# Two attention mixers: rope rows swapped by SBUF to SBUF copies, and the latent up projection packed by parts

## The chip, the core and the metric

The kernel runs on one core of one Trainium2 chip. The time is that of the device, in microseconds, for one launch, as the median of repeated runs. It is lower for a better kernel. The input is one sequence of 512 tokens with 1024 features, in fp32.

## What the kernel computes

One layer with a gated delta rule and windowed attention comes first (not touched here), and then two identical layers, each made of a feed-forward block, a mixer, a second feed-forward block and a gated embedding block. The mixer is what changes. Cut to what matters, with x normalised, it is:

```
p = x @ w_in_2[l]                       # 1024 -> 384 latents, 32 shared rope key, 1024 dilated q and k, 512 dilated v
q_lat, kv_lat = norm(p[:, 0:256]), norm(p[:, 256:384])
q  = (q_lat @ w_q_up).reshape(512, 8, 96)       # per head 64 plain features and 32 that are rotated
kv = (kv_lat @ w_kv_up).reshape(512, 8, 128)    # per head 64 key features and 64 value features
key of head h   = [kv[:, h, 0:64], rope(p[:, 384:416])]      # 96 features; the rope part is shared by the heads
query of head h = [q[:, h, 0:64],  rope(q[:, h, 64:96])]
latent heads : softmax(causal(query . key / sqrt(96))) @ value, 8 heads
dilated heads: 8 heads of 64 features, 4 tiles of queries and 4 of keys (two heads to a tile), all rotated
rope(a) = a * cos + swapped(a) * signed sin     # swapped: rows i and i ^ 16 (latent) or i ^ 32 (dilated) change places
```

Features lie on the 128 partitions and tokens along the free axis, so a rotation has to exchange rows between partitions.

## The kernel before

All projections run as sums of three products (`matmul3`, lines 227 to 229): weights and activations are split into a high part (`w_hi`, made by ScalarE at line 181) and a rest (`w_lo`, made by VectorE at line 189). Weights come in granules of 128 by 1024 numbers (512 KB), fetched by SyncE at line 171 into one of four raw slots. Four split granules are kept. `w_split`, `w_used` and similar semaphores count granules, and every engine walks its own written order; there is no scheduler. In the last section of the program (`chain`) each engine simply runs the mixer's method of its name (`sp`, `pool`, `pe`, `act`, `dve`).

The mixer has three parts on TensorE:

- **Twelve input tiles** t, 24 products each. From t = 6 each is preceded by one rope swap. VectorE drains a tile by multiplying it with the reciprocal root (line 2655).
- **Twenty up tiles** j: 8 query tiles (one head each, 96 of 128 rows used, 6 products), 8 key tiles (64 of 128 rows used, 3 products), 4 value tiles (3 products). The first eleven are preceded by one swap each. ScalarE drains each tile (lines 2526, 2528 and 2530) into `qh`, `kh` and `vm`.
- **64 attention items** (`score`, `turn`, `weigh`), with 32 pieces of the dilated value product (`values`) between the first 32 of them.

A rotation ("rope") r goes as follows. TensorE multiplies the raw tile by a permutation matrix (`swap`, line 2330) into PSUM, GpSimd multiplies the raw tile by the cosines into `by_cos` (line 2310), VectorE multiplies the swapped tile by the signed sines into `by_sin` (line 2612) and adds the two (line 2617). There are 17 of them in each mixer: r = 0 the shared key, 1 to 4 dilated queries, 5 to 8 dilated keys, 9 to 16 the eight latent query heads. `by_cos` and `by_sin` have two slots each. GpSimd starts `by_cos` of r when the sum of r - 2 is done.

The first score waits for all up tiles to be drained. Here are its waits and those of `turn`, which end with the last rope:

```
if i < 16:
    pe.wait_ge(*self.rope_added(10 + head))
if i == 0:
    pe.wait_ge(*self.up_drained(self.UPS))
    pe.wait_ge(*self.key_copied(1))
```

Of the kernel before, what the change touches and what calls it, by code (L numbers as in the profile page):

```python
# [22 lines left out]
ALU = mybir.AluOpType  # L23
# [39 lines left out]
def _small(*fields):  # L63
# [17 lines left out]
    ("ffn0", 44 + 24), ("mix_in", 12), ("up", 4), ("mix_v", 4), ("mix_out", 8), ("ffn1", 44 + 24), ("ple", 3), ("ple_gate", 8))  # L81
# [2130 lines left out]
class Mixer:  # L2212
# [13 lines left out]
    def __init__(self, kit, layer, delta_gain, leave, b):  # L2226
        self.kit, self.layer, self.b, self.made, self.leave = kit, layer, b, leave.makes, leave
        self.g0, self.u0, self.v0, self.o0 = kit.take(self.TILES), kit.take(4), kit.take(4), kit.take(KD)
# [36 lines left out]
    def up_ready(self, j):  # L2265

        last_of = {3: 1, 7: 2, 15: 3, 19: 4}
        if j in last_of:
            return self.kit.w_used, self.u0 + last_of[j]
        return self.up_done(j + 1 - sum(e < j for e in last_of))  # L2270

    def rope_job(self, r):

        b = self.b
        if r == 0:
            return b["k_rope"][:, :], [(slice(0, P), b["k_rope"][:, :])], "swap_16", 0, self.drained(4)
        if r < 5:
            raw = self.kit.delta[:, 2 * (r - 1)]
            return raw, [(slice(0, HD), raw[0:HD]), (slice(HD, P), self.kit.delta[HD:P, 2 * (r - 1) + 1])], "swap_32", 1, self.drained(r + 4)
        if r < 9:  # L2280
            return b["kd"][:, r - 5], [(slice(0, P), b["kd"][:, r - 5])], "swap_32", 1, self.drained(r + 4)
        return b["qh"][:, r - 9], [(slice(0, P), b["qh"][:, r - 9])], "swap_16", 0, self.up_drained(r - 8)
# [8 lines left out]
    def sp(self, sp):  # L2291
# [5 lines left out]
        fetch_ahead(kit, sp, self.g0, self.TILES + 8 + KD)  # L2297

    def pool(self, pool):
# [5 lines left out]
        for r in range(self.ROPES):  # L2305
# [14 lines left out]
    def pe(self, pe):  # L2320
# [3 lines left out]

        def swap(r):
            src, _, name, _, ready = self.rope_job(r)
            pe.wait_ge(*ready)
            if r >= 2:
                pe.wait_ge(*self.sin_done(r - 1))
            pe.matmul(kit.banks[4 + r % 2][:, :], kit.square(name), src, start=True, stop=True).then_inc(self.swapped.sem, 1)  # L2330

        self.entry.pe(pe)
        for t in range(2, self.TILES):
# [19 lines left out]
            if t >= 6:  # L2353
                swap(t - 6)
# [6 lines left out]
        for j in range(self.UPS):  # L2361
            if j + 6 < self.ROPES:
                swap(j + 6)
            pe.wait_ge(*(self.drained(7 + j) if j < 4 else self.up_drained(j - 3)))
            if j in (0, 8):
                pe.wait_ge(*self.lat_rested(2 if j == 0 else 3))
            if j in (0, 4, 8, 16):
                pe.wait_ge(kit.w_split, u0 + (0, 4, 8, 16).index(j) + 1)
            out = self.up_bank(j)[:, :]
            if j < 8:  # L2370
                for k in range(2):
                    last = matmul3(pe, out, kit.w_tile(u0 + j // 4, j % 4 * 2 + k), [x[:, k] for x in lat], k == 0, k == 1)
            elif j < 16:
                last = matmul3(pe, out, kit.w_tile(u0 + 2, j - 8), [x[:, 2] for x in lat], True, True)
            else:
                tok = slice((j - 16) * P, (j - 15) * P)
                last = matmul3(pe, out, [x[:, 2, tok] for x in lat], kit.w_wide(u0 + 3, 0), True, True)
            last.then_inc(kit.w_used if j in (3, 7, 15, 19) else self.up_done.sem, 1)

        def score(i):  # L2380
# [40 lines left out]
        def turn(i):  # L2421
# [3 lines left out]
            else:  # L2425
                pe.wait_ge(*self.rope_added(self.ROPES))
# [64 lines left out]
    def act(self, act):  # L2491
# [26 lines left out]
        for j in range(self.UPS):  # L2518
            if j in (0, 4, 8, 16):
                kit.w_make_hi(act, self.u0 + 3 + (0, 4, 8, 16).index(j))  # L2520
            act.wait_ge(*self.up_ready(j))
            bank = self.up_bank(j)
            if j == 4:
                act.wait_ge(*self.lat_rested(3))
            if j < 8:
                last = act.activation(b["qh"][:, j], bank[:, :], ACT.Copy)
            elif j < 16:
                last = act.activation(b["kh"][0:HD, j - 8], bank[0:HD, :], ACT.Copy)
            else:
                last = act.activation(b["vm"][:, j - 16, :, 0:HD], bank[:, :].rearrange("p (h n) -> p h n", h=8), ACT.Copy)  # L2530
# [68 lines left out]
    def dve(self, dve):  # L2599
# [4 lines left out]
        def rope(r):  # L2604
            _, parts, _, table, _ = self.rope_job(r)
            dve.wait_ge(*self.swapped(r + 1))
# [5 lines left out]
            dve.tensor_tensor(by_sin, kit.banks[4 + r % 2][:, :], b["cos_sin"][:, 2 + table], ALU.mult).then_inc(  # L2612
# [341 lines left out]
def layer_buffers(kit):  # L2954
# [24 lines left out]
    place(EXIT_UNIT, ("probs_t", [P, 2, 512]))  # L2979
# [40 lines left out]
def pack_weights(x):  # L3020
# [34 lines left out]
    for l in range(LAYERS):  # L3055
# [11 lines left out]
        q_up = np.zeros((256, 8, P), w.dtype)  # L3067
        q_up[:, :, 0:96] = x["w_q_up_2"][l].reshape(256, 8, 96)
# [111 lines left out]
```

## Time and profile before

| | value |
|---|---|
| median of 3 runs | 3229.46 us (3228.98 to 3229.71) |
| the profiled execution, its own time | 3230.68 us |
| its span, first to last instruction | 3228.8 us |
| TensorE busy | 2996.9 us, 93% |
| VectorE, ScalarE, GpSimd busy | 49%, 36%, 10% |
| mean granted TensorE clock | 0.962 |
| SyncE's queue | 433 weight fetches of 512 KB |

The profiled execution took 1.2 us more than the median of the runs, and 1.9 us of its time lie outside the span. Busy time is what an engine spent in instructions. In the chain of work that ended last each moment is given to one engine, the one that everything behind it waited for. A matmul's record overlaps the next one's, so the chain's pieces, and not the records, tell what a product costs. "Idle before" a row tells how long that engine had nothing to do before it and what released it.

### The profile page before, as it was taken

Reading aid. Unit: us, or ns where it says so; the run is one execution under the profiler, and the core shown is the slowest. Engines: PE = TensorE matmul, PEld = TensorE weight load, DVE = VectorE, ACT = ScalarE, POOL = GpSimd, SP = SyncE. Lnnn points to the kernel's source line nnn. Section 1 sums busy time; section 2 is a strip of 40 time slices with the busy share of each in tenths; the row PEclk is TensorE's granted clock in tenths of the full one; section 3 lists DMA queues with packets and bytes.
Section 4 is the critical chain, followed back from the end, with each engine's and each line's share of the span. In section 5 each row is a group of like instructions: output and inputs, shape, how many; then the busy total and the mean of one; then the engine's idle time right before and its main releaser. Section 6 shows DMA issues by size and latency. Waiting matters only on the chain.

```text
span 3228.8 us, 39471 instructions
## 1 busy us (share of the span) xinstructions
PE 2996.9 (93%) x15600; PEld 2504.5 (78%) x15600; DVE 1580.6 (49%) x2589; ACT 1177.5 (36%) x1885; POOL 311.5 (10%) x293
## 2 busy tenths in 40 slices
PE   5988799889799999998999999899999989999997
PEld 2877689867678888766788888788888667888886
DVE  5725465442544443754464434654436645544336
ACT  4324544233232332434443323533324345423224
POOL 0001077600000000120100000000000200000000
PEclk8999899999899999998999999999999999999998
DMA  5220100012223232310123232133332201232331
GB/s 214 71 73 1 64 1 1 1 53 78 72 87 102 93 103 92 103 48 27 40 81 98 95 105 92 54 110 98 98 105 98 65 14 40 72 98 94 102 97 54
DMA packets 66854, 241.90 MB, mean 75 GB/s; under 512 B 7408, under 2 KB 9584, under 8 KB 66032
## 3 DMA queue, kind: packets, MB, share of 16 engines
q1 hardware_dynamic: 66672, 239.38, 22.8%
q8 instruction: 125, 2.05, 0.3%
q14 instruction: 57, 0.47, 0.0%
HBM read 236.21 MB, written 3.15 MB: 74 GB/s over the span
## 4 chain that ended last, share of the span: by engine, by line
PE 64%; DVE 4%; ACT 2%; issue 1%; DVEq 0%; ACTq 0%
PE pair L227 19%; PE pair L229 18%; PE pair L228 18%; PE pair L2417 2%; PE pair L2392 2%; PE pair L376 1%; PE pair L2429 1%; PE pair L2330 1%; ACT w_hi_at L181 1%; DVE rstd_at L500 1%; DVE work_at L331 1%; DVE w_lo_at L189 0%; ACT probs_t_at L2547 0%; DVE h_lo_at L340 0%; PE pair L518 0%
## 5 line engine op out<-in xcount | busy, mean ns | idle before, releaser
L227 PE MATMUL pair<-h_hi_at,w_hi_at 128*128 128x512 f32 (+1 forms) x2048 | 790.1, 386 | 35.2 <-DVE h_lo_at L340 30.8
L228 PE MATMUL pair<-h_lo_at,w_hi_at 128*128 128x512 f32 (+1 forms) x2048 | 761.7, 372 | 0.0
L229 PE MATMUL pair<-h_hi_at,w_lo_at 128*128 128x512 f32 (+1 forms) x2048 | 761.5, 372 | 0.0
L189 DVE TENSOR_TENSOR w_lo_at<-w_raw,w_hi_at 128x1024 fp32r<-128x1024 f32 x350 | 440.7, 1259 | 465.3 <-ACT w_hi_at L181 465.2
L181 ACT ACTIVATE w_hi_at<-w_raw 128x1024 fp32r<-128x1024 f32 x350 | 367.3, 1054 | 549.7 <-PE pair L229 538.4
L227 PEld LDWEIGHTS pair<-h_hi_at,w_hi_at 128*128 128x128 f32 x2048 | 391.0, 191 | 113.7 <-DVE h_lo_at L340 36.3
L228 PEld LDWEIGHTS pair<-h_lo_at,w_hi_at 128*128 128x128 f32 x2048 | 391.5, 191 | 70.5 <-issue 3.4
L229 PEld LDWEIGHTS pair<-h_hi_at,w_lo_at 128*128 128x128 f32 x2048 | 391.2, 191 | 65.3
L2181 DVE TENSOR_TENSOR work_at<-pair,rstd_at 128x512 f32<-128x512 f32 (+1 forms) x184 | 122.1, 667 | 362.9 <-PE pair L229 362.8
L227 PE MATMUL pair<-a_hi_at,w_hi_at 128*128 128x512 f32 (+1 forms) x792 | 290.1, 366 | 0.0
L228 PE MATMUL pair<-a_lo_at,w_hi_at 128*128 128x512 f32 (+1 forms) x792 | 289.4, 365 | 0.0
L229 PE MATMUL pair<-a_hi_at,w_lo_at 128*128 128x512 f32 (+1 forms) x792 | 289.4, 365 | 0.0
L508 POOL TENSOR_TENSOR exit_work_at<-exit_work_at 128x512 f32<-128x512 f32 x44 | 63.1, 1435 | 2222.2 <-ACT exit_work_at L470 2222.0
L227 PE MATMUL pair<-h_hi,w_hi 128*128 128x512 f32 (+1 forms) x432 | 166.3, 385 | 29.2 <-DVE h_lo L264 21.5
L2157 ACT ACTIVATE work_at<-work_at 128x512 f32<-128x512 f32 x88 | 55.7, 633 | 334.6 <-DVE work_at L2181 334.6
L227 PEld LDWEIGHTS pair<-a_hi_at,w_hi_at 128*128 128x128 f32 x792 | 149.4, 189 | 24.3
L228 PEld LDWEIGHTS pair<-a_lo_at,w_hi_at 128*128 128x128 f32 x792 | 149.3, 189 | 24.3
L229 PEld LDWEIGHTS pair<-a_hi_at,w_lo_at 128*128 128x128 f32 x792 | 149.3, 189 | 24.0
L228 PE MATMUL pair<-h_lo,w_hi 128*128 128x512 f32 (+1 forms) x432 | 163.6, 379 | 0.0
L229 PE MATMUL pair<-h_hi,w_lo 128*128 128x512 f32 (+1 forms) x432 | 163.1, 378 | 0.0
L189 DVE TENSOR_TENSOR w_lo<-w_raw,w_hi 128x1024 fp32r<-128x1024 f32 x59 | 71.9, 1225 | 185.0 <-ACT w_hi L181 184.9
L181 ACT ACTIVATE w_hi<-w_raw 128x1024 fp32r<-128x1024 f32 x59 | 62.1, 1060 | 216.5 <-PE pair L229 195.7
(394 smaller groups left out, 4371.0 us busy)
## 6 DMA issues: line engine op xcount, KB each, us to landing
w_raw<-in_weights SPq DMA_DIRECT2D x433, 512.0 KB, 3.5
residual<-in_x SPq DMA_DIRECT2D x1, 2048.0 KB, 11.7
cos_sin_at<-rope_table SPq DMA_DIRECT2D x2, 1024.0 KB, 5.3
out<-residual SPq DMA_DIRECT2D x16, 128.0 KB, 1.7
ctx_in<-in_ctx SPq DMA_DIRECT2D x1, 1024.0 KB, 12.9
rope_table<-zb SPq DMA_DIRECT2D x1, 1024.0 KB, 4.9
mask_at<-in_layer_masks SPq DMA_DIRECT2D x2, 512.0 KB, 6.4
levels<-in_levels SPq DMA_DIRECT2D x1, 896.0 KB, 7.3
```

What stands on the lines that cost most here:

```text
L181: eng.activation(self.w_hi[:, g % self.split].rearrange("p k n -> p (k n)"), self.w_raw[:, slot], ACT.Copy).then_inc(self.w_hi_ready, 1)
L189: eng.tensor_tensor(self.w_lo[:, g % self.split].rearrange("p k n -> p (k n)"), self.w_raw[:, g % RAW], self.w_hi[:, g % self.split].rearr ...
L227: pe.matmul(out, sh, mh, start=start, stop=False)
L228: pe.matmul(out, sh, ml, start=False, stop=False)
L229: return pe.matmul(out, sl, mh, start=False, stop=stop)
L331: dve.scalar_tensor_tensor(self.buf[:, (at + t) % 4], self.leave.source(t, half), self.delta_gain(t), kit.rstd[:, c], ALU.mult, ALU.mult). ...
L376: pe.matmul(self.kit.banks[self.SUM_BANK[half]][:, 0:HALF], self.kit.square("ones"), self.sq[:, n % 4], start=(t == 0), stop=(t == KD - 1) ...
L508: pool.tensor_tensor(self.total, self.total, self.sq[:, t % 2], ALU.add).then_inc(self.out_added.sem, 1)
L2157: act.activation(self.gate[:, f % 2], self.gate[:, f % 2], ACT.Silu).then_inc(self.gate_silu.sem, 1)
L2181: last = dve.tensor_tensor(dst[:, f % 2, c], bank, kit.rstd[:, c], ALU.mult)
L2392: pe.matmul(kit.banks[1 + i % 3][:, 0:w], q, k, start=True, stop=True).then_inc(self.scored.sem, 1)
L2417: last = pe.matmul(kit.banks[6 + i % 2][:, 0:HD + 1], b["probs_t"][:, i % 2, c * P:(c + 1) * P], v[:, c, head], start=(c == 0), stop=(c == ...
```

## The change

Three things change together in each of the two mixers.

1. **Rotations.** SyncE swaps rows with small copies from SBUF to SBUF, written straight into `by_sin`: 2 copies of 16 rows for r = 0, 4 copies of 32 rows for r = 1 to 8, 8 copies of 16 rows for r = 9 and 10. VectorE multiplies `by_sin` in place. TensorE swaps nothing any more.
2. **Packing.** The 32 rope features of four heads share one tile, so the query's rope part takes 2 up tiles (6 products each) instead of being a part of 8. The 64 plain features of two heads share a tile: 4 key tiles (3 products) and 4 query tiles (6 products). With 4 value tiles there are 14 up tiles and 11 rotations. ScalarE drains a tile of two heads in two halves of 64 rows. One weight granule less is fetched and split in each mixer. The rotated rows then have to be moved to each head's rows 64 to 95 of `qh`, by 8 more copies of 32 rows on SyncE (`move`).
3. **Waits.** The first score waits for these 8 moves, and no score or turn waits for a single rope any more. VectorE splits three of the four `mix_v` granules behind the last rope.

```
-    TILES, UPS, ITEMS = 12, 20, 64
+    TILES, UPS, ITEMS = 12, 14, 64
-    ROPES = 17
+    ROPES, UP_ENDS = 11, (5, 9, 13)
...
-        return b["qh"][:, r - 9], [(slice(0, P), b["qh"][:, r - 9])], "swap_16", 0, self.up_drained(r - 8)
+        return b["q_rope"][:, r - 9], [(slice(0, P), b["q_rope"][:, r - 9])], 16, 0, self.up_drained(r - 8)
+
+    def swap(self, sp, r):
+        src, _, rows, _, ready = self.rope_job(r)
+        sp.wait_ge(*ready)
+        if r >= 2:
+            sp.wait_ge(*self.rope_added(r - 1))
+        out = self.b["by_sin"][:, r % 2]
+        for at in range(*(HD, HD + 32, rows) if r == 0 else (0, P, rows)):
+            there = at ^ rows
+            sp.dma_start(out[at:at + rows], src[there:there + rows]).then_inc(self.swapped[r % 2].sem, 16)
+
+    def move(self, sp, r):
+
+        sp.wait_ge(*self.rope_added(r + 1))
+        for i in range(4):
+            sp.dma_start(self.b["qh"][HD:HD + 32, 4 * (r - 9) + i], self.b["q_rope"][32 * i:32 * i + 32, r - 9]).then_inc(
+                self.moved.sem, 16)
...
-        fetch_ahead(kit, sp, self.g0, self.TILES + 8 + KD)
+        for g in range(self.g0 + RAW, self.o0 + KD + RAW):
+            kit.w_fetch(sp, g)
+            t = g - RAW - 3 - self.g0
+            if 3 <= t < self.TILES:
+                self.swap(sp, t - 3)
+            if g == self.o0:
+                for r in (9, 10):
+                    self.swap(sp, r)
+                for r in (9, 10):
+                    self.move(sp, r)
...
-                pool.wait_ge(*self.sin_done(r + 1))
+                pool.wait_ge(*self.swaps_until(r))
...
-            if t >= 6:
-                swap(t - 6)
...
-            if i < 16:
-                pe.wait_ge(*self.rope_added(10 + head))
             if i == 0:
                 pe.wait_ge(*self.up_drained(self.UPS))
                 pe.wait_ge(*self.key_copied(1))
+                pe.wait_ge(*self.moved(128))
...
-            dve.tensor_tensor(by_sin, kit.banks[4 + r % 2][:, :], b["cos_sin"][:, 2 + table], ALU.mult).then_inc(
+            dve.tensor_tensor(by_sin[turned], by_sin[turned], b["cos_sin"][turned, 2 + table], ALU.mult).then_inc(
                 self.sin_done.sem, 1)
...
-        makes = {6: self.u0 + 3, 9: self.v0, 12: self.v0 + 1, 16: self.v0 + 2}
         for r in range(6, self.ROPES):
-            if r in makes:
-                kit.w_make_lo(dve, makes[r])
             rope(r)
-        kit.w_make_lo(dve, self.v0 + 3)
+            if r == 7:
+                kit.w_make_lo(dve, self.v0)
+        for g in range(self.v0 + 1, self.v0 + 4):
+            kit.w_make_lo(dve, g)
```

SyncE's queue, before: the end of the feed-forward fetches, the tables of the first mixer, and everything up to the second mixer.

```order
L585 UNCONDITIONAL_BRANCH
L171 DMA w_raw<-in_weights 128x1024 x68
L2295 DMA cos_sin_at_8585<-rope_table 128x2048
L2296 DMA mask_at_8582<-in_layer_masks 128x1024
L171 DMA w_raw<-in_weights 128x1024 x175
```

SyncE's queue now, from the swap of the last dilated key tile (r = 8) to the fetches that follow the first mixer's moves.

```order
L2292 DMA by_sin_at_8602<-kd_at_8581 32x512 x4
L171 DMA w_raw<-in_weights 128x1024
L2292 DMA by_sin_at_8602<-q_rope_at_8599 16x512 x16
L2301 DMA qh_at_8583<-q_rope_at_8599 32x512 x8
L171 DMA w_raw<-in_weights 128x1024 x158
```

The queue held weight fetches alone. Now 58 small copies stand in it in each mixer, and the last 24 of them follow one fetch (that of granule `o0`).

VectorE, before: from the drain of input tile 11 (`kd`) on, with the split of granule `u0 + 3`, ropes 6 to 8, the split of `v0`, and rope 9 (`qh`).

```order
L2655 TENSOR_TENSOR kd_at_8581<-pair,rstd_at_8570 128x512
L189 TENSOR_TENSOR w_lo_at_8574<-w_raw,w_hi_at_8573 128x1024
L2612 TENSOR_TENSOR by_sin_at_8601<-pair,cos_sin_at_8585 128x512
L2617 TENSOR_TENSOR kd_at_8581<-by_cos_at_8600,by_sin_at_8601 128x512
L2612 TENSOR_TENSOR by_sin_at_8601<-pair,cos_sin_at_8585 128x512
L2617 TENSOR_TENSOR kd_at_8581<-by_cos_at_8600,by_sin_at_8601 128x512
L2612 TENSOR_TENSOR by_sin_at_8601<-pair,cos_sin_at_8585 128x512
L2617 TENSOR_TENSOR kd_at_8581<-by_cos_at_8600,by_sin_at_8601 128x512
L189 TENSOR_TENSOR w_lo_at_8574<-w_raw,w_hi_at_8573 128x1024
L2612 TENSOR_TENSOR by_sin_at_8601<-pair,cos_sin_at_8585 128x512
L2617 TENSOR_TENSOR qh_at_8583<-by_cos_at_8600,by_sin_at_8601 128x512
```

VectorE now, from behind the drain of input tile 11 to the last three splits, the items' first operation coming next.

```order
L2630 TENSOR_TENSOR by_sin_at_8602<-by_sin_at_8602,cos_sin_at_8585 128x512
L2635 TENSOR_TENSOR kd_at_8581<-by_cos_at_8601,by_sin_at_8602 128x512
L2630 TENSOR_TENSOR by_sin_at_8602<-by_sin_at_8602,cos_sin_at_8585 128x512
L2635 TENSOR_TENSOR kd_at_8581<-by_cos_at_8601,by_sin_at_8602 128x512
L189 TENSOR_TENSOR w_lo_at_8574<-w_raw,w_hi_at_8573 128x1024
L2630 TENSOR_TENSOR by_sin_at_8602<-by_sin_at_8602,cos_sin_at_8585 128x512
L2635 TENSOR_TENSOR kd_at_8581<-by_cos_at_8601,by_sin_at_8602 128x512
L2630 TENSOR_TENSOR by_sin_at_8602<-by_sin_at_8602,cos_sin_at_8585 128x512
L2635 TENSOR_TENSOR q_rope_at_8599<-by_cos_at_8601,by_sin_at_8602 128x512
L2630 TENSOR_TENSOR by_sin_at_8602<-by_sin_at_8602,cos_sin_at_8585 128x512
L2635 TENSOR_TENSOR q_rope_at_8599<-by_cos_at_8601,by_sin_at_8602 128x512
L189 TENSOR_TENSOR w_lo_at_8574<-w_raw,w_hi_at_8573 128x1024 x3
```

Eleven ropes with four splits between them have become five ropes with one split between the second and the third, and the multiplication reads SBUF where it read PSUM.

ScalarE now, over the up tiles: the last splits for the input tiles, then the drains. Before, it drained 8 query tiles, 8 key tiles and 4 value tiles with one instruction each.

```order
L181 ACTIVATE w_hi_at_8573<-w_raw 128x1024 x3
L2541 ACTIVATE q_rope_at_8599<-pair 128x512 x2
L2545 ACTIVATE kh_at_8584<-pair 64x512 x8
L181 ACTIVATE w_hi_at_8573<-w_raw 128x1024
L2545 ACTIVATE qh_at_8583<-pair 64x512 x8
L181 ACTIVATE w_hi_at_8573<-w_raw 128x1024
L2547 ACTIVATE vm_at_8591<-pair 128x8x64 x4
L181 ACTIVATE w_hi_at_8573<-w_raw 128x1024
```

The drains are 22 instead of 20, for 14 tiles instead of 20, and the key tiles come ahead of the plain query tiles.

## Rows read from the trace of the kernel before

**Rows 1.** The page: the span, and busy time by engine.
```profile
span 3228.8 us, 39471 instructions
PE 2996.9 (93%) x15600; PEld 2504.5 (78%) x15600; DVE 1580.6 (49%) x2589; ACT 1177.5 (36%) x1885; POOL 311.5 (10%) x293
```

**Rows 2.** The chain that ended last: start us, us, what; last two rows second mixer.
```profile
1344.97 0.86 PE pair L2330 x2
...
1382.93 0.86 PE pair L2330 x2
1383.80 0.23 PE pair L227
...
1392.45 1.06 ACT w_hi_at L181
...
1406.06 2.04 PE pair L2330 x2
...
1420.55 1.10 PE pair L2392 x2
...
2532.46 0.86 PE pair L2330 x2
...
2570.44 1.10 PE pair L2392 x2
```

**Rows 3.** ScalarE in order of time: start us, us, instruction [idle before, releaser].
```profile
1413.55 4.03 ACT L2528 ACTIVATE kh_at<-pair 64x512 f32<-64x512 f32 x6 [0.96 <-PE pair L229]
...
1418.43 2.02 ACT L2530 ACTIVATE vm_at<-pair 128x512 f32<-128x512 f32 x4
```

**Rows 4.** VectorE in order of time, first mixer.
```profile
1371.89 0.69 DVE L2655 TENSOR_TENSOR kd_at<-pair,rstd_at 128x512 f32<-128x512 f32 x1
1372.50 1.62 DVE L189 TENSOR_TENSOR w_lo_at<-w_raw,w_hi_at 128x1024 fp32r<-128x1024 f32 x1
1374.04 0.68 DVE L2612 TENSOR_TENSOR by_sin_at<-pair,cos_sin_at 128x512 f32<-128x512 f32 x1
1374.75 1.39 DVE L2617 TENSOR_TENSOR delta_at<-by_cos_at,by_sin_at 64x512 f32<-64x512 f32 x2
...
1385.99 0.69 DVE L2617 TENSOR_TENSOR kd_at<-by_cos_at,by_sin_at 128x512 f32<-128x512 f32 x1
...
1387.31 1.33 DVE L2617 TENSOR_TENSOR kd_at<-by_cos_at,by_sin_at 128x512 f32<-128x512 f32 x1
...
1393.54 1.23 DVE L189 TENSOR_TENSOR w_lo_at<-w_raw,w_hi_at 128x1024 fp32r<-128x1024 f32 x1 [2.92 <-ACT w_hi_at L181]
```

**Rows 5.** GpSimd in order of time, beside the slow sum of rows 4.
```profile
1386.82 1.27 POOL L2310 TENSOR_TENSOR by_cos_at<-kd_at,cos_sin_at 128x512 f32<-128x512 f32 x1 [4.43 <-DVE kd_at L2617]
```

**Rows 6.** SyncE's queue in order of time: what an issue takes there.
```profile
3.68 1.14 SPq L866 DMA_DIRECT2D squares<-in_squares  x1
4.86 0.70 SPq L867 DMA_DIRECT2D qb<-in_positions  x1
...
1298.68 0.33 SPq L2295 DMA_DIRECT2D cos_sin_at<-rope_table  x1
1299.05 0.43 SPq L2296 DMA_DIRECT2D mask_at<-in_layer_masks  x1
1299.53 1.10 SPq L171 DMA_DIRECT2D w_raw<-in_weights  x2
```

**Rows 7.** The page's DMA issues: KB each, median us from issue to landing.
```profile
w_raw<-in_weights SPq DMA_DIRECT2D x433, 512.0 KB, 3.5
...
out<-residual SPq DMA_DIRECT2D x16, 128.0 KB, 1.7
...
small<-in_small SPq DMA_DIRECT2D x1, 144.5 KB, 2.2
```

**Rows 8.** Stretches: us, busy (x) of PE, PEld, DVE, ACT, POOL; granted clock, DMA.
```profile
1406.00:1411.00 5.00, 4.95 (x8) 2.60 (x9) 4.49 (x5) 0.59 (x1) 2.55 (x3) 0.50 0.33 105
...
818.00:824.00 6.00, 5.83 (x14) 4.57 (x15) 1.25 (x2) 0.00 (x0) 0.00 (x0) 0.50 0.52 175
```

More of the change, by code:

```diff
@@ L2227, in __init__ @@
         self.kit, self.layer, self.b, self.made, self.leave = kit, layer, b, leave.makes, leave
[L2228 removed]
+        self.g0, self.u0, self.v0, self.o0 = kit.take(self.TILES), kit.take(3), kit.take(4), kit.take(KD)
         self.entry = Entry(kit, self.g0, gains(kit, layer, 2), delta_gain, leave)
@@ L2265, in up_ready @@
     def up_ready(self, j):
[L2267 to L2270, printed above, removed]
+        if j in self.UP_ENDS:
+            return self.kit.w_used, self.u0 + self.UP_ENDS.index(j) + 1
+        return self.up_done(j + 1 - sum(e < j for e in self.UP_ENDS))
     def rope_job(self, r):
@@ L2323, in pe @@
         ident = kit.square("ident")
[L2325 to L2330, printed above, removed]
         self.entry.pe(pe)
@@ L2361, in pe @@
         for j in range(self.UPS):
[L2362 to L2363 removed]
             pe.wait_ge(*(self.drained(7 + j) if j < 4 else self.up_drained(j - 3)))
[L2365 removed]
+            if j in (0, 2):
                 pe.wait_ge(*self.lat_rested(2 if j == 0 else 3))
[L2367 to L2368 removed]
+            if j in (0, 6, 10):
+                pe.wait_ge(kit.w_split, u0 + (0, 6, 10).index(j) + 1)
             out = self.up_bank(j)[:, :]
[L2370 removed]
+            if j < 2 or 6 <= j < 10:
                 for k in range(2):
[L2372 to L2378 removed]
+                    last = matmul3(pe, out, kit.w_tile(u0 + (j >= 6), (j if j < 2 else j - 6) * 2 + k), [x[:, k] for x in lat], k == 0, k == 1)
+            elif j < 6:
+                last = matmul3(pe, out, kit.w_tile(u0, j + 2), [x[:, 2] for x in lat], True, True)
+            else:
+                tok = slice((j - 10) * P, (j - 9) * P)
+                last = matmul3(pe, out, [x[:, 2, tok] for x in lat], kit.w_wide(u0 + 2, 0), True, True)
+            last.then_inc(kit.w_used if j in self.UP_ENDS else self.up_done.sem, 1)
         def score(i):
@@ L2518, in act @@
         for j in range(self.UPS):
-            if j in (0, 4, 8, 16):
-                kit.w_make_hi(act, self.u0 + 3 + (0, 4, 8, 16).index(j))
+            if j in (0, 6, 10):
+                kit.w_make_hi(act, self.v0 + (0, 6, 10).index(j))
             act.wait_ge(*self.up_ready(j))
             bank = self.up_bank(j)
-            if j == 4:
+            if j == 8:
                 act.wait_ge(*self.lat_rested(3))
[L2525 to L2528, printed above, removed]
+            if j < 2:
+                last = act.activation(b["q_rope"][:, j], bank[:, :], ACT.Copy)
+            elif j < 10:
+                dst, h = (b["kh"], 2 * (j - 2)) if j < 6 else (b["qh"], 2 * (j - 6))
+                for i in range(2):
+                    last = act.activation(dst[0:HD, h + i], bank[i * HD:(i + 1) * HD, :], ACT.Copy)
             else:
-                last = act.activation(b["vm"][:, j - 16, :, 0:HD], bank[:, :].rearrange("p (h n) -> p h n", h=8), ACT.Copy)
+                last = act.activation(b["vm"][:, j - 10, :, 0:HD], bank[:, :].rearrange("p (h n) -> p h n", h=8), ACT.Copy)
             last.then_inc(self.up_drained.sem, 1)
@@ L3115, in pack_small @@
     inv = lambda dim: (np.float32(10000.0) ** (-np.arange(0, dim, 2, dtype=np.float32) / np.float32(dim))).astype(np.float32)
-    rotated = (row >= HD) & (row < HD + 32)
-    put("inv_mla", np.where(rotated, inv(32)[row % 16], 0).astype(np.float32))
+    put("inv_mla", inv(32)[row % 16])
     put("sign_mla", np.where(row % 32 < 16, -1, 1).astype(np.float32))
```

35 lines of the change are left out of this document (18 added, 17 removed).

## The prediction

> **What bounds the kernel now.** I read the page first: TensorE is busy for 2996.9 of 3228.8 us [rows 1], so most of the program goes at its pace. The next view is the chain that ended last, over the first mixer. There the swaps stand on the path: a swap is one instruction and two passes, and takes 0.86 us of the chain, against 0.23 us for one product [rows 2]. Six input tiles with six swaps take 1382.93 - 1344.97 = 37.96 us. The up tiles, from the swap ahead of the first to the first score, take 1420.55 - 1382.93 = 37.6 us [rows 2]. In them stand 84 products (84 x 0.23 = 19.3 us) and 11 swaps (9.5 us), 28.8 in all. The remaining 8.8 us are two stalls, where a swap waits for a rope, the rope waits behind a split of VectorE, and the split waits for ScalarE's high part (the first begins at 1392.45 [rows 2], and VectorE sat idle for 2.92 us there [rows 4]), and what follows the second: the clock is at 0.50 from 1406 to 1411 [rows 8], and a swap takes 2.04 us [rows 2]. The second mixer has the same picture: 2570.44 - 2532.46 = 38.0 us [rows 2].
>
> **The input tiles.** Without the six swaps of t = 6 to 11, tile 11 ends 6 x 0.86 = 5.2 us earlier, at 1377.8. Does anything else hold TensorE there? The rows of a tile are drained four to five tiles ahead of need, so VectorE's backlog has room. The copies are issued at t = 3 to 11 and wanted three tiles later. SyncE waits in order at each, up to the rope two before, so the weight fetches behind it start later than before; but a fetch lands in 3.5 us [rows 7] and is wanted several tiles (5.5 us each) on. I cost this at nothing. If that cover is gone, the splits come late and TensorE waits for them.
>
> **The up tiles on TensorE and ScalarE.** 60 products take 13.8 us: TensorE is done at 1391.6 at the earliest. ScalarE now drains 22 times. Six drains of 64 rows took 4.03 us while TensorE fed them, four back to back took 2.02 us, so 0.5 us each when nothing is waited for [rows 3]. From 1377.8 ScalarE has three splits of 1.06 us [rows 2] and 22 x 0.5 = 11.0 us, 14.2 in all, and its first drain can't start before the first six products (1.4 us) are through. Its early drains of two-head tiles are slower than TensorE, which has four banks. I put the last drain at 16 us after tile 11, or 1393.8. This is the floor for the first score: 26.8 us earlier than 1420.55.
>
> **The rope chain on VectorE and SyncE.** It is what I expect to end last. Terms: a drain 0.6 (start to start of the first two rows), a split 1.2 alone and 1.6 in the backlog, a rope 1.4 (0.7 and 0.7), or 2.1 with its sum in two halves [rows 4]. A sum of two SBUF tiles took 1.33 us instead of 0.69 when it met `by_cos` on GpSimd, which runs for 1.27 us [rows 4, 5]. The multiplication now also reads two SBUF tiles, so I add 0.7 us wherever the next `by_cos` is released at the same moment. An issue on SyncE: starts 0.37 and 0.48 us apart, I take 0.42; the bounds are 0.33 and 1.14 [rows 6]. No copy of 32 or 64 KB from SBUF to SBUF stands in the trace. From issue to landing the smallest transfers took 1.7 us (128 KB out) and 2.2 us (144.5 KB in), the weights 3.5 us; I take 2.0, with 1.3 and 3.5 as ends [rows 7].
>
> - VectorE is at its split at 1372.5, as before, since it works off a backlog there. Split 1.6, rope 4 2.1 + 0.7, drain 0.6, split 1.6, rope 5 1.4, drain of tile 11 0.6: 1381.1, of which rope 5 ends at 1380.5.
> - Rope 6: held by `by_cos` of 7, ends 1383.2. Swap 7, issued from 1380.5, lands 3 x 0.42 + 2.0 = 3.3 later. Rope 7 is held again and ends at 1385.9.
> - Split of `v0` to 1387.1. Rope 8 (its swap landed at 1386.5), ends 1388.5, or 1389.1 with half of a hold.
> - Only that split lets SyncE issue the fetch of `o0` (1387.1), then the eight copies of swap 9 (1387.6 to 1390.5, landed 1392.5), and the eight of swap 10 (1390.9 to 1393.9, landed 1395.9). Rope 9 ends at 1393.9, rope 10 at 1397.3.
> - The moves of rope 9 are issued by 1396; the four of rope 10 from 1397.3 to 1398.6, landed 1400.6. The first score at 1400.7.
>
> So the first score comes 19.8 us earlier in the first mixer and, by the same sum from 2570.44, 20.2 in the second: 40 us. The three splits behind rope 10 (3.6 us) end by 1401, hidden under the score and its wait for the moves, and the high part of the last one is ready by 1395. If they weren't, the first mask would be late.
>
> The Trainium skill (DMA: Bandwidth & Descriptors, the anatomy of one DMA and the bandwidth table) speaks against small copies: a fixed 2.0 us each plus bytes over 436 GB/s, and transfers under 64 KB are dominated by descriptors. By its fit, given for another issuing path, a landing would be an estimated 2.15 us, and the sum 0.5 us less gain in each mixer. No run so far shows such a copy.
>
> **The clock.** TensorE would stand from 1391.6 to 1400.7. After a stand of 3.6 us before 1406 the granted clock was 0.50, the lower of its two levels, for 5 us; elsewhere it was 0.50 throughout 818 to 824 with TensorE busy [rows 8]. Such a stretch at half rate loses 2.5 to 3 us. Before, this loss lay inside the up tiles; now it comes behind the first score, where items and value products fill TensorE. I take 2.5 us in each mixer. The sum: 40 - 5 = 35 us. Against the profiled execution's own 3230.7 us that gives 3195.7, and its 1.2 us over the median taken off, **3194.5 us**.
>
> **The rivals.**
>
> - *The copies hide* (12%). Issues of 0.33 us and landings of 1.3 save 20 x 0.09 + 3 x 0.7 = 3.9 us, and no holds by GpSimd another 2: the score is then at ScalarE's floor, with a short stand and little loss of clock. 26.8 + 27.2 = 54 us less: 3176. For it: copies are a quarter of the smallest transfer seen. Against it: three landings and 20 issues in sequence.
> - *The copies are dear* (20%). At 0.70 us an issue and 3.5 us a landing the chain grows by 20 x 0.28 + 3 x 1.5 = 10 us in each mixer: 15 us less in all, 3214. For it: the first issues of the program took 0.70 and 1.14 us [rows 6], and swap 9 stands behind a 512 KB fetch.
> - *SyncE's queue makes it slower* (4%). The mechanism is the same in-order queue: 20 issues on the path between the split of `v0` and the score. The gain is gone when the score is later than 1418, which is 17.4 us beyond my sum: with landings of 3.5 us, 20 issues of 1.06 us each. At 1.5 us an issue and 2.0 a landing the chain grows by 21.6 us, and with 17.4 given back to each mixer the kernel is 8 us slower, 3238. One row of 1.14 us [rows 6] speaks for it, all those of the mixer against.
> - *Time given back by the items* (2%): they go no faster for starting earlier, and a late weight fetch for the output (its granules now leave after the moves) could cost what was won. They are wanted only from item 36, over 60 us on. It would end near 3229.
>
> The forecast itself has the remaining 62%; with its terms between their nearer bounds it reaches from 3183 to 3206. Less than 0.2% (6.5 us) is about what a measurement of this kernel can't tell from no change. Faster by more than that: 62 + 12 + 19, 93%. Within: 3%. Slower: 4%. The range for 8 in 10 takes in most of the first rival and part of the second: 3178 to 3209.
>
> **What the changed kernel's profile would show.** Right: no permutation products; input tiles 5.5 us apart; 60 products for the up tiles; a stand of TensorE of about 9 us ahead of the first score that ends with a landing of `qh`, at some 23 us behind tile 11; SyncE's copies 0.4 us apart; the granted clock at 0.50 for some 5 us behind the score. The step on issue and landing is wrong if swap 9 lands much before or after 5 us from the fetch of `o0`. The step on ScalarE is wrong if the last drain comes later than the moves. The prediction as a whole is wrong if input tiles stay 6.3 us apart, because splits or copies hold them, or if the items behind take longer than they did.

## The result, and the profile of the changed kernel

The changed kernel takes 3204.96 us (median of 4 runs, 3203.5 to 3207.73), the kernel before 3229.22 us in the same series (3227.48 to 3229.71). The ratio is 0.9927, 95% interval 0.991 to 0.9944: 24.3 us faster. The forecast was 3194.5 in a range from 3178 to 3209. The direction and the place were right. The gain was put at 35 us, so a third of it is missing.

The page of the changed kernel, against [rows 1]:

```profile
span 3201.7 us, 39245 instructions
PE 2953.7 (92%) x15484; PEld 2480.1 (77%) x15484; DVE 1559.9 (49%) x2563; ACT 1177.6 (37%) x1887; POOL 302.2 (9%) x281
```

TensorE has 43 us less work, and the span is 27.1 us shorter. The chain of the first mixer, from inside swap 9 to the first score, answers to [rows 2] (start us, us, what):

```profile
1387.30 0.46 SPq L2292
1387.76 0.04 issue
1387.80 0.59 SPq L2292
1388.39 0.04 issue
...
1396.66 1.95 DMA by_sin_at<-q_rope_at
...
1398.64 0.70 DVE by_sin_at L2630
...
1399.36 0.70 DVE q_rope_at L2635
...
1400.08 0.51 SPq L2301
...
1401.90 2.00 DMA qh_at<-q_rope_at
...
1404.03 2.05 PE pair L2409 x2
```

This is the forecast's chain, piece by piece: copies of swap 9 and 10, a landing, rope 10, moves, a landing, the score. Landings take 1.95 and 2.00 us, counted from the start of the last issue, where 2.0 was taken. The issues are dearer: a record of 0.59 us and 0.04 us between two, 0.63 us from start to start (1387.80, then 1388.43), where 0.42 was taken from [rows 6].

SyncE's queue in order of time, from swap 7 on (the first row). The last fetch ahead of the sixteen copies is that of `o0`:

```profile
1379.21 2.51 SPq L2292 DMA_DIRECT2D by_sin_at<-kd_at  x4
1381.77 0.58 SPq L171 DMA_DIRECT2D w_raw<-in_weights  x1
1382.44 2.41 SPq L2292 DMA_DIRECT2D by_sin_at<-kd_at  x4
1386.82 0.33 SPq L171 DMA_DIRECT2D w_raw<-in_weights  x1
1387.25 10.00 SPq L2292 DMA_DIRECT2D by_sin_at<-q_rope_at  x16
1397.30 5.19 SPq L2301 DMA_DIRECT2D qh_at<-q_rope_at  x8
```

VectorE over the same time, against [rows 4] (in brackets the idle time before a row and what ended it):

```profile
1358.38 2.44 DVE L2645 SCALAR_TENSOR_TENSOR lat_buf_at<-lat_at,small,rstd_lat_at 128x512 f32<-128x512 f32 x2
...
1372.10 1.78 DVE L2630 TENSOR_TENSOR by_sin_at<-by_sin_at,cos_sin_at 128x512 f32<-128x512 f32 x1
...
1375.94 1.88 DVE L189 TENSOR_TENSOR w_lo_at<-w_raw,w_hi_at 128x1024 fp32r<-128x1024 f32 x1
1377.74 0.68 DVE L2630 TENSOR_TENSOR by_sin_at<-by_sin_at,cos_sin_at 128x512 f32<-128x512 f32 x1
...
1384.24 0.69 DVE L2630 TENSOR_TENSOR by_sin_at<-by_sin_at,cos_sin_at 128x512 f32<-128x512 f32 x1 [2.39 <-DMA by_sin_at<-kd_at]
...
1393.57 0.69 DVE L2630 TENSOR_TENSOR by_sin_at<-by_sin_at,cos_sin_at 128x512 f32<-128x512 f32 x1 [4.35 <-DMA by_sin_at<-q_rope_at]
```

The multiplication takes 0.68 us alone and 1.78 us when GpSimd's `by_cos` runs beside it, the split 1.22 alone and 1.88 so. The first row is a pair of operations on the latents that met `by_cos` too. In the kernel before it did not:

```profile
1361.25 1.40 DVE L2627 SCALAR_TENSOR_TENSOR lat_buf_at<-lat_at,small,rstd_lat_at 128x512 f32<-128x512 f32 x2
```

ScalarE, against [rows 3]:

```profile
1377.79 4.88 ACT L2545 ACTIVATE kh_at<-pair 64x512 f32<-64x512 f32 x8
...
1383.64 4.87 ACT L2545 ACTIVATE qh_at<-pair 64x512 f32<-64x512 f32 x8
...
1389.49 2.07 ACT L2547 ACTIVATE vm_at<-pair 128x512 f32<-128x512 f32 x4
```

GpSimd's `by_cos` beside the 1.78 us product is the first row below, against [rows 5]; the page's transfers are the next ones (KB each, median us to landing), against [rows 7]:

```profile
1370.97 2.36 POOL L2339 TENSOR_TENSOR by_cos_at<-kd_at,cos_sin_at 128x512 f32<-128x512 f32 x1
```

```profile
by_sin_at<-kd_at SPq DMA_DIRECT2D x32, 64.0 KB, 2.0
...
by_sin_at<-q_rope_at SPq DMA_DIRECT2D x32, 32.0 KB, 2.0
qh_at<-q_rope_at SPq DMA_DIRECT2D x16, 64.0 KB, 2.0
```

And the stretches around the first score, against [rows 8] (us, busy of PE, PEld, DVE, ACT, POOL, granted clock, DMA share, GB/s):

```profile
1390.00:1403.00 13.00, 0.00 (x0) 0.00 (x0) 5.71 (x7) 2.49 (x5) 0.63 (x1) 0.54 0.28 69
1403.00:1408.00 5.00, 3.97 (x8) 2.59 (x9) 1.34 (x4) 0.72 (x1) 0.00 (x0) 0.50 0.89 286
1408.00:1413.00 5.00, 5.00 (x29) 3.77 (x27) 1.12 (x6) 1.94 (x5) 0.00 (x0) 0.98 0.10 42
```

TensorE stands for 14.5 us (from 1389.5 to 1404.03), and starts the items at 1.2 GHz (0.50).

**One zero point for all kernels.** The same code ahead of the first mixer ends up to 5 us apart from one profiled execution to another, so absolute times of two traces can't be subtracted. All marks below count from the start of the last product of input tile 11, T0 (1373.96 in the changed kernel, 1382.5 in the kernel before). "Item 8" is VectorE's first drain of the dilated values, which comes with item 8; both mixers are given.

| kernel | median us | first score | first mask | item 8 |
|---|---|---|---|---|
| before | 3229.2 | 38.0, 38.4 | 40.0, 40.4 | 54.7, 55.1 |
| changed | 3205.0 | 30.1, 29.0 | 32.1, 31.1 | 48.8, 48.7 |
| pack_only | 3196.7 | 21.0, 20.9 | 23.0, 23.0 | 39.3, 37.7 |
| copies_only | 3221.8 | 20.3, 20.3 | 38.6, 38.3 | 54.8, 56.6 |
| double_issue | 3239.4 | 46.2, 45.5 | 48.3, 47.6 | 65.3, 64.7 |
| fetch_behind | 3202.8 | 28.2, 27.7 | 30.2, 29.8 | 47.9, 46.4 |
| direct_adds | 3203.4 | 28.3, 27.2 | 31.6, 30.5 | 47.8, 46.0 |
| pe_9_10 | 3194.4 | 23.3, 23.0 | 25.4, 25.1 | 42.1, 42.3 |
| pe_7_10_direct | 3194.8 | 24.8, 24.9 | 26.9, 26.9 | 41.6, 41.6 |
| filler | 3206.8 | 30.3, 29.6 | 32.1, 31.7 | 48.6, 49.0 |
| filler_64 | 3205.2 | 29.9, 29.9 | 31.0, 31.0 | 46.5, 46.5 |
| half_wait | 3184.9 | 19.8, 18.7 | 24.4, 23.3 | 38.6, 38.4 |
| half_wait_late_splits | 3185.0 | 19.7, 18.6 | 22.0, 20.9 | 38.0, 38.4 |

Before and pack_only also carry six swaps ahead of T0, which is 5.2 us in each mixer (6 x 0.86, [rows 2]). The changed kernel's gain from this table: 2 x 5.2 + (54.7 - 48.8) + (55.1 - 48.7) = 22.7 us, against 24.3 in the medians. The items behind item 8 gave nothing back. From the first score to item 8 the kernel before takes 16.7 us in both mixers, the changed kernel 18.7 and 19.7: 5.0 us more in all.

### The profile page after: what moved, and what is told of

It is laid out like the page before. It is cut to its first block, busy times and chain, and to the rows that moved or that the text cites. A ratio compares the mean times of both kernels' runs of the same rounds, so it can differ in the third digit from the quotient of the medians.

```text
span 3201.7 us, 39245 instructions
## 1 busy us (share of the span) xinstructions
PE 2953.7 (92%) x15484; PEld 2480.1 (77%) x15484; DVE 1559.9 (49%) x2563; ACT 1177.6 (37%) x1887; POOL 302.2 (9%) x281
## 4 chain that ended last, share of the span: by engine, by line
PE 63%; DVE 4%; ACT 3%; issue 1%; SPq 0%; DMA 0%; DVEq 0%; ACTq 0%
PE pair L227 19%; PE pair L228 18%; PE pair L229 18%; PE pair L2434 2%; PE pair L2409 2%; PE pair L376 1%; PE pair L2444 1%; ACT w_hi_at L181 1%; DVE rstd_at L500 1%; DVE work_at L331 1%; DVE w_lo_at L189 0%; ACT probs_t_at L2564 0%; DVE h_lo_at L340 0%; SPq L2292 0%; DVE residual L336 0%
## 5 line engine op out<-in xcount | busy, mean ns | idle before, releaser
L227 PEld LDWEIGHTS pair<-a_hi_at,w_hi_at 128*128 128x128 f32 x792 | 149.4, 189 | 24.4
```

The lines of the kernel that those rows point to most:

```text
L227: pe.matmul(out, sh, mh, start=start, stop=False)
```

## The experiments

The theory: the first score waits for a chain of rope, issue and landing on VectorE and SyncE; 20 issues and the holds by GpSimd are what was costed too low. The rivals: the landings, the clock after the stand, ScalarE's drains.

**Each half of the change alone.** `pack_only` packs by parts and moves with copies, but TensorE makes all eleven swaps. Its edit to the changed kernel:

```
+            if t >= 6:
+                pe_swap(t - 6)
...
+            if j + 6 < self.ROPES:
+                pe_swap(j + 6)
...
-            dve.tensor_tensor(by_sin[turned], by_sin[turned], ...
+            dve.tensor_tensor(by_sin[turned], kit.banks[4 + r % 2][turned, :], ...
```

> The changed kernel with all 11 swaps of a mixer back on TensorE (a permutation product into PSUM) and only the 8 moves left on SyncE: the packing alone. My theory is that the in-order copies ahead of the first score set its time. By it the input tiles end 5.2 us later again (six swaps), five ropes follow with no landing between them, and the first score comes at ScalarE's floor, some 17 to 18 us after tile 11, where the changed kernel has 29.6: 6 to 7 us less in each mixer, and a shorter stand of TensorE: 3188 us, 3182 to 3195. The rival, that the removed permutation products are what won the time, gives 2 x 9.5 us back: 3224.

`copies_only` is the kernel before with its 17 ropes and 20 up tiles, all swaps as copies:

```
+        after = {self.v0 + 3: (9, 10), self.o0: (11, 12), self.o0 + 1: (13, 14, 15, 16)}
...
+            for r in after.get(g, (t - 3,) if 3 <= t < self.TILES else ()):
+                self.swap(sp, r)
...
-            if j + 6 < self.ROPES:
-                swap(j + 6)
```

> The kernel before (20 up tiles, 17 ropes) with every swap done by copies on SyncE: 4 of 32 rows for a dilated rope, 2 of 16 rows for the key and for each query head. No moves. Ropes 9 to 16 then take turns in two slots, each about 0.64 us of issue, 2.0 of landing and 1.4 of VectorE behind the rope two before: some 2.1 us a rope and 34 us from tile 11 to the last one, against 44.8 in the kernel before by the same start. I expect 10 us less in each mixer: 3209, 3200 to 3220. A rival that sees copies as the whole gain expects 3205 or less; one that sees them as a loss expects over 3229.

Measured: pack_only 3196.65 (ratio 0.9897, 0.9883 to 0.9912), which is 8 us better than the whole change (its slowest run, 3201.8, is faster than the changed kernel's fastest, 3203.5). copies_only 3221.8 (0.9971, 0.9959 to 0.9982), 13 us worse than expected. In copies_only the first score is early, since it waits for one head, but VectorE then goes through the rest of the 17 ropes before the first mask (38.6 us), and most of them wait for a landing:

```profile
1401.20 3.00 DMA by_sin_at<-qh_at
1404.22 0.69 DVE by_sin_at L2621
...
1405.69 0.51 SPq L2293
...
1406.24 1.99 DMA by_sin_at<-qh_at
1408.26 0.69 DVE by_sin_at L2621
```

So packing is worth 33.9 us alone (3230.5 before in that series), the copies 8.7 us alone, and on top of the packing the copies cost 8 to 10 us (8.3 by the medians, 9.6 by each series' own kernel before). There the 10.4 us won on the input tiles are paid back, and more, on the chain ahead of the score. pack_only lacks more than issues and landings: its multiplication reads PSUM again, as in the kernel before. What the issues alone cost is the next run's question.

**The price of an issue.** `double_issue` moves the same bytes with twice the copies of ropes 9 and 10 (32 and 16 instead of 16 and 8):

```
-        for at in range(*(HD, HD + 32, rows) if r == 0 else (0, P, rows)):
+        step = rows // 2 if r >= 9 else rows
+        for at in range(*(HD, HD + 32, rows) if r == 0 else (0, P, step)):
```

> The changed kernel with each copy of the last two swaps and each move cut into two copies of half the rows: same bytes, 20 more issues on the path of each mixer. If SyncE's issue (0.635 us from start to start in the trace) sets the pace there, 12.7 us more in each mixer: 3230, 3224 to 3236. If the landing or the bytes set it, less than 5 us more in all: 3205 to 3210.

Measured 3239.42 (1.0031, 1.0019 to 1.0042): 34.5 us over the changed kernel. SyncE's queue in it:

```profile
1388.70 21.48 SPq L2293 DMA_DIRECT2D by_sin_at<-q_rope_at  x32
1410.22 10.29 SPq L2302 DMA_DIRECT2D qh_at<-q_rope_at  x16
```

The median lies above the range that was expected. The score is 16.2 and 16.6 us later. From the first issue of swap 9 to the last move, the queue now holds 48 issues where it held 24: 16 more for the swaps at 0.667 us and 8 more for the moves at 0.632 make 15.7 us, and the other swap copies are 0.035 us dearer each. The expectation counted 20: it left out rope 9's moves, which in the changed kernel lie under the landing of swap 10, and are too many for that when doubled. A copy of half the bytes took no less to issue (16 KB: 0.62 us and 0.05 between; 32 and 64 KB: 0.59 and 0.04). This settles the issue cost: the number of copies counts, not their size.

**The fetch ahead of swap 9.** `fetch_behind` issues the fetch of `o0` behind the moves, so that swap 9 no longer waits for the split of `v0`:

```
-            kit.w_fetch(sp, g)
+            if g != self.o0:
+                kit.w_fetch(sp, g)
...
                 for r in (9, 10):
                     self.move(sp, r)
+                kit.w_fetch(sp, g)
```

> The changed kernel with the one weight fetch that stands ahead of swap 9 (it waits for the split of the first value granule) issued behind the moves instead. Swap 9 can then go when rope 7 is added: by the trace 1385.65 instead of 1387.25, 1.6 us earlier in each mixer, if the copies are on the path: 3201.7. If the fetch also slowed the copies on the DMA engines, more: 3198. If something else holds the first score, nothing: 3205.

Measured 3202.83 (0.9914, 0.9899 to 0.9929). The score comes 1.9 and 1.3 us earlier, just as much as swap 9 starts earlier; in the medians 2.1 us, which the intervals do not tell from none. The run also shows what a weight fetch does to the copies behind it. In the changed kernel swap 9's first copies, issued 0.43, 0.98 and 1.61 us behind the fetch of `o0`, land after 3.08, 2.79 and 2.51 us, and only the sixth, at 3.5 us, after 1.95. Without that fetch the first three take 2.19, 2.28 and 1.95 us (second mixer 2.24, 1.94 and 1.96, against 3.16, 2.97 and 2.58). The last copy, for which VectorE waits, lands after 1.95 us in both.

**No moves.** `direct_adds` sums straight into the heads, in four pieces of 32 rows:

```
-        return b["q_rope"][:, r - 9], [(slice(0, P), b["q_rope"][:, r - 9])], ...
+        return b["q_rope"][:, r - 9], [(slice(32 * i, 32 * i + 32), b["qh"][HD:HD + 32, 4 * (r - 9) + i]) for i in range(4)], ...
...
-                pe.wait_ge(*self.moved(128))
+                pe.wait_ge(*self.rope_added(11))
```

> The changed kernel without the 8 moves: VectorE writes each of the four 32-row sums of ropes 9 and 10 straight to rows 64 to 95 of its head, four sums of 0.7 us where one was. On the path 3 x 0.7 = 2.1 us more of VectorE, against 3 issues and a landing (3.95 us) less: 1.8 us less in each mixer, 3201.3, 3198 to 3204. If sums across row groups cost more than 0.7 us each, the gain is gone: 3205 or more.

Measured 3203.44 (0.9917, 0.9904 to 0.9931). The score is 1.7 and 1.8 us earlier, the first mask only 0.5, since the splits stand behind the longer sums. A sum of 32 rows takes VectorE as long as one of 128:

```profile
1404.15 2.78 DVE L2633 TENSOR_TENSOR qh_at<-by_cos_at,by_sin_at 32x512 f32<-32x512 f32 x4
```

**Two swaps back to TensorE.** `pe_9_10` leaves swaps 0 to 8 as copies and gives TensorE the last two (the edit of pack_only, for r = 9 and 10).

> The changed kernel with only the swaps of ropes 9 and 10 (the packed query rope parts, 16 of the copies) back on TensorE, which stands idle there; swaps 0 to 8 and the moves stay copies. Theory (the copies behind the last split set the first score): ropes 9 and 10 follow rope 8 at once, and the eight moves end some 22.8 us behind tile 11 instead of 29.6: 6.8 us less in each mixer, 3191, 3186 to 3196. The rival, that VectorE's backlog sets it: within 2 us of 3205.

Measured 3194.41 (0.989, 0.9877 to 0.9904): the sixteen issues and one landing are gone, the score comes at 23.3 us, and what it waits for is the eight moves. Ahead of them its chain has a landing of 3.12 us, that of swap 8. In `pe_7_10_direct`, swaps 7 to 10 are TensorE's, and there are no moves:

> The changed kernel with the swaps of ropes 7 to 10 on TensorE and the sums of 9 and 10 written straight to the heads, so that no copy stands behind tile 11: the version that the theory points to. By the sum: rope 8 ends 11 us behind tile 11, ropes 9 and 10 at 18, the three splits at 21.3, where the first mask begins (31.7 in the changed kernel); ScalarE's last drain at 17. 10 us less in each mixer and about 1 of the clock: 3182, 3176 to 3190. Below 3188 it also beats the packing alone, if that comes out as forecast.

Measured 3194.75 (0.9891, 0.9877 to 0.9904), 13 us over the expectation, which had ScalarE's last drain at 17 us and left the bound to VectorE. TensorE, rows with a stand before them:

```profile
1379.33 1.12 PE L2366 MATMUL pair<-kd_at,squares 128*128 128x512 f32 x2 [0.36 <-DVE kd_at L2692]
1383.03 1.13 PE L2366 MATMUL pair<-kd_at,squares 128*128 128x512 f32 x2 [1.19 <-DVE kd_at L2692]
1385.81 1.10 PE L2366 MATMUL pair<-q_rope_at,squares 128*128 128x512 f32 x2 [0.95 <-DVE by_sin_at L2649]
```

The swaps stand in TensorE's order ahead of the up tiles and wait for VectorE, which is late in its backlog: swaps 7 and 8 for its drains of input tiles 10 and 11, swap 9 for the multiplication of rope 7. ScalarE's drains begin later for it, and they end last:

```profile
1394.12 4.87 ACT L2564 ACTIVATE qh_at<-pair 64x512 f32<-64x512 f32 x8
...
1399.97 2.06 ACT L2566 ACTIVATE vm_at<-pair 128x512 f32<-128x512 f32 x4
```

T0 is 1377.2 there, so the last drain ends at 24.8 us, the moment of the score. In pe_9_10, where swaps 7 and 8 are copies and TensorE does not wait for them, it ends at 18.3 us; in pack_only, with all eleven on TensorE, it ends at 20.9, again the moment of the score. The wait for the moves is gone, and ScalarE's later drains take its place. For ropes 9 and 10 a product was the better swap: pe_9_10 differs from the changed kernel in these two swaps alone and is 10.5 us faster in the medians. For ropes 7 and 8, and for all the earlier ones, the times don't decide: pe_9_10, pe_7_10_direct and pack_only lie between 3194.4 and 3196.7, and their intervals overlap.

**The clock.** `filler` has TensorE make 48 products that nobody reads ahead of the first score (`filler_64`: 64), so that it doesn't stand:

```
+        for i in range(48):
+            pe.matmul(kit.banks[5][:, :], h[0][:, i % KD, 0:P], h[0][:, i % KD], start=True, stop=True)
```

> The changed kernel with 48 products of 512 columns into an unused bank between the last up tile and the first score of each mixer, where TensorE waits anyway (12.8 us in the trace; the products take 11 us at 0.23). It leaves nothing out, and nothing reads what they give. If the stand of TensorE costs the clock (0.50 for about 4.5 us behind the first score), this wins 2 to 3 us in each mixer: 3200, 3198 to 3202. If the granted clock there doesn't matter since the items wait for other engines, it stays at 3205.

Measured 3206.79 (0.9922, 0.9909 to 0.9936): nothing won. But 48 were too few. TensorE stood for the last 3.88 us, and the granted clock still fell (0.63 from 1408 to 1412, 0.50 from 2545 to 2550 in the second mixer):

```profile
1392.24 11.05 PE L2399 MATMUL pair<-h_hi_at 128*128 128x512 f32 x48
1407.17 1.67 PE L2412 MATMUL pair<-kh_at,qh_at 96*128 96x512 f32 x2 [3.88 <-DMA qh_at<-q_rope_at]
```

> The changed kernel with 64 idle products ahead of the first score instead of 48, whose sums nobody reads; 48 of them ended 3.9 us before the score and the clock still fell. My theory: a stand of TensorE ahead of the score costs about 2 us by the clock (from the first score to the first value drain 18.7 us in the changed kernel, 16.7 us in the version with swaps 7 to 10 on TensorE, whose clock stayed at 1.00). Then the clock is 1.00 through the score, that stretch takes 16.7 us, and the time is 3201 (3198 to 3204), 4 us under the changed kernel. The rival, that the clock costs nothing here or falls anyway: 3205 and 18.7 us.

Measured 3205.2 (0.9922, 0.9907 to 0.9937), where 3201 was expected and 3205 was the rival's. Now no stand is left and the granted clock is 1.00 throughout:

```profile
1404.00:1408.00 4.00, 4.00 (x19) 3.34 (x18) 3.81 (x4) 0.00 (x0) 0.00 (x0) 1.00 0.39 98
1408.00:1412.00 4.00, 4.00 (x16) 2.63 (x16) 1.00 (x4) 1.02 (x2) 0.00 (x0) 1.00 0.91 332
```

From the score to item 8 it takes 16.6 us, against 18.7 and 19.7 in the changed kernel, and item 8 comes 2.2 us earlier in each mixer. (The last of the 64 products ends at the moment of the score, so the score itself may wait for them: in the second mixer it is 1.0 us later.) So the loss by the clock is of the size that was forecast, 2 to 3 us in each mixer. The time of the whole kernel doesn't show the 4.4 us. Each median is good to some 5 us, and in the profiled executions the stretch behind the second mixer's item 8 took 643.9 us with the filler and 640.1 without, where the others lie between 639.9 and 643.5. Whether the filler costs something there or this is chance stays open.

**What the experiments point to.** TensorE's swaps for ropes 9 and 10 only, and no waiting for heads that aren't needed yet: items 0 to 7 use heads 0 to 3. `half_wait` sums rope 9 into those heads in four pieces, and lets only item 8 wait for rope 10's four moves. It also puts the turned probabilities of every second item into slot 2 of `probs_t`, not slot 1; no run has that alone. Of its edit, the waits:

```
             if i == 0:
                 pe.wait_ge(*self.up_drained(self.UPS))
                 pe.wait_ge(*self.key_copied(1))
-                pe.wait_ge(*self.moved(128))
+                pe.wait_ge(*self.rope_added(10))
+            if i == 8:
+                pe.wait_ge(*self.moved(64))
```

> Swaps 9 and 10 on TensorE, rope 9 summed straight into heads 0 to 3 in four pieces, rope 10 summed whole and moved by 4 copies that only item 8 waits for (head 4 is the first that needs them). My theory: what held the version with swaps 9 and 10 on TensorE was the 8 moves, 6.4 us between rope 10 and the first score. The first score then waits for rope 9 and for ScalarE alone and comes 18.9 us behind the last product of input tile 11 (there 23.3), but the first mask stands behind three splits on VectorE, at 24 us (there 25.4). So 3191 (3188 to 3195). The rival, that the items go no faster for an earlier score: 3194.4 as in that version.

`half_wait_late_splits` also moves two of VectorE's three splits behind masks 1 and 3:

> As the version that waits for half of the heads, and VectorE splits the third and fourth granule of the dilated value weights behind the second and the fourth mask, not ahead of the first. My theory: VectorE is then the last to be ready, and the first mask comes 2.3 us earlier, about 21.8 us behind input tile 11: 3187 (3183 to 3191). The rival: the splits are wanted at the third and fifth item and hold VectorE there for as long, so nothing is won over the version before it, 3191.

Measured 3184.92 (0.9857, 0.9841 to 0.9874) and 3184.95 (0.9858, 0.9843 to 0.9873): both beat both kernels, 20 us under the changed one and 46 under the one before in their series. The first ends 6 us under its expectation: score and mask come about where they were put, and the clock, 0.77 and 0.80 around them, is back at 1.00 by 1404, so that the mask is followed by item 8 in 14.2 and 15.1 us, where pe_9_10 takes 16.7 and 17.2. The second gives no more: its first mask is 2.4 us earlier as expected, but item 8 only 0.6 and 0.0. In its chain the products behind the score are what counts, at the low clock:

```profile
1396.17 1.17 PE pair L2432 x2
1397.34 0.43 PE pair L227
...
```

The mask was no longer the bound there; TensorE was. Both chains still run through swap 8, whose last copy lands 3.28 and 3.11 us after its issue:

```profile
1388.24 3.28 DMA by_sin_at<-kd_at
```

A kernel with the same waits and all swaps on TensorE, which has no such landing, was not run.

## Why the prediction was right, and where it was off

The measured time lies in the forecast's range, 10.5 us above its 3194.5. Which chain ends last, and why, was right. Two terms of the sum were too small: the steps between issues, and what stands ahead of swap 9.

- **Input tiles: right.** They come 5.44 us apart with no swap (ScalarE's splits at 1369.01 and 1374.45), where 5.5 was forecast. Neither copies nor fetches held them.
- **Which chain ends last: right**, in all its links (the chain above).
- **The term that was too small: the chain of issues.** "An issue on SyncE: starts 0.37 and 0.48 us apart, I take 0.42." It is 0.63, and 0.55 for the second copy of a group. The 20 issues on the path are 18 steps from start to start (15 in the swaps, 3 in the last moves), 7.6 us at 0.42. They took 1396.66 - 1387.25 = 9.41 and 1401.90 - 1400.08 = 1.82 us, 11.2 in all: 3.7 us more in each mixer, about 7 of the missing 11. The two rows behind the 0.42 [rows 6] are loads of 1 MB and 512 KB from DRAM; a run of small copies from SBUF was nowhere in the trace of before. The bound of 0.70 in the rival "copies are dear" was closer than the value taken. double_issue confirms the term at twice the count. The forecast's own sign shows it too: swap 9 lands 6.7 us from the fetch of `o0`, not 5.
- **The start of swap 9: late by 3.2 us in the first mixer and 2.1 in the second.** Forecast 9.8 us behind tile 11 (1387.6 - 1377.8), measured 1387.25 - 1374.3 = 13.0 (tile 11 ends 0.3 behind T0) and 11.9. In both mixers VectorE is some 2.1 us behind the forecast when rope 5 ends. The forecast has VectorE at its split at 1372.5 "as before", which is 5.3 us ahead of tile 11's end at 1377.8. In the changed kernel this split starts at 1370.97, 3.3 us ahead: 2.0 us were lost already, so "as before" is what did not hold. Most of them were lost in rows that met `by_cos`: 2.44 us for 1.40 in the pair shown above, 1.91 for 1.22 and 1.91 for 1.61 in two splits (a third got faster, 1.22 for 1.62). GpSimd's clearing ahead of these `by_cos` now waits for a copy's landing and not for VectorE's multiplication, so `by_cos` meets other operations than before. The rest of the 3.2 us, in the first mixer alone, is swap 7. Its last copy, issued at 1381.13 while a 512 KB fetch was in flight (1377.82 to 1382.94), took 3.08 us to land; in the second mixer it took 2.04.
- **The landing otherwise: right**, 1.95 us for 32 KB and 2.00 for 64 KB where no fetch is in flight. The Trainium skill (DMA: Bandwidth & Descriptors, the anatomy of one DMA) has a fixed 2.0 us, and its fit, given for another issuing path, an estimated 2.15 for 64 KB; the trace agrees with the fixed part and is 0.15 us under the fit.
- **ScalarE's floor: right in kind, short by 1 us.** A half drain takes 0.61 us back to back (4.88 for 8), not 0.5; the last ends at 1391.56, 17.3 us behind tile 11 and not 16. In the changed kernel it hides, with 12 us to spare; it is the bound in pack_only and pe_7_10_direct.
- **The clock: right in the trace.** It is 0.50 for 4.2 us behind the first score of the first mixer and 6.4 us in the second, and from the score to item 8 2.0 and 3.0 us are lost against before, where 2.5 was taken for each. By the time of the whole kernel filler_64 doesn't confirm it.
- **Sum.** Forecast from tile 11 to the first score 22.9 us, measured 29.7: 3.2 for the late start and 3.7 for the steps between issues. In the second mixer it is 2.1 and 3.7. 6.8 and 5.8 us make 12.6 us of shortfall; the measured gain is 11 less than forecast. The difference is within what a median leaves open.
- **Rivals.** "The copies hide" ended 29 us too low, since neither its issue of 0.33 us nor its landing of 1.3 came about. "SyncE's queue makes it slower" did not come about in this kernel, but double_issue, whose chain grew by 16 us, is it: slower than before by 0.31%. The forecast put the turning point at 17.4 us beyond its sum; the changed kernel had used 6.8 of them, and 16 more crossed it. "The copies are dear" (3214) is as near to the measured time as the forecast (3194.5): its 0.70 us for an issue nearly came about, its 3.5 us for a landing only for copies with a weight fetch in flight, and of these only swap 7 of the first mixer stood on the path. Nothing was given back by the items behind.

## What to carry to other kernels

Count the DMA issues that stand in sequence on the path, and price each at what a run of such copies takes in a queue, not at a single issue in the trace; from 16 to 64 KB the bytes made no difference to that. A product in the path of the busiest engine can be cheaper than a copy off it, when the copy's latency lands in front of the next stage: keep the last swaps on the engine. Whether copies for the steps with slack are then worth having was not settled here (3194.4 with them, 3196.7 without, intervals overlapping). And before shortening a wait, ask whether all that it waits for is needed yet: here, waiting for half of the heads was part of the version that won 20 us more.

## What the runs showed of the hardware

- Copies from SBUF to SBUF on SyncE's queue, from issue to issue: 0.63 us at 64 KB and 32 KB (0.55 for the second of a group), 0.667 at 16 KB.
- From issue to landing they take 1.9 to 2.05 us, and up to 3.5 us with a 512 KB fetch of the same queue in flight (3.51 for the last copy of swap 8 in the changed kernel). Behind a fetch the landing gets shorter copy by copy: 3.08, 2.79, 2.51, 2.38, 2.17, 1.95 us. fetch_behind, which takes that fetch away, has 2.19, 2.28, then 1.95 or 1.94.
- VectorE and GpSimd hold each other up when both read SBUF: a multiplication of 0.69 us becomes 1.46 to 1.78, a split of 1.22 becomes 1.9, and `by_cos` of 1.29 becomes 2.36. The Trainium skill (SBUF — State Buffer, who interferes with whom) says that a VectorE instruction with two SBUF inputs contends with a GpSimd instruction that reads SBUF, over a port pair that the two engines share; the rows agree. The multiplication that reads PSUM took 0.68 us in the kernel before even where `by_cos` ran beside it (1388.57, `by_cos` from 1388.79). Moving the swapped tile from PSUM to SBUF put one more operation of the first kind into each rope.
- An operation of VectorE on 32 rows takes as long as one on 128 (0.69 us for 512 numbers in each row).
